# Gated linear attention in a two-block forward pass: the chunk states of the second pair move into VectorE's turn of the first

## The reference, cut to what matters

```python
def step(S, inp):
    qj, kj, vj, laj = inp
    bcum = jnp.cumsum(laj, axis=2)
    ...
    o = jnp.einsum('bhls,bhse->bhle', attn, vj) + jnp.einsum('bhld,bhde->bhle', qj * jnp.exp(bcum), S)
    btot = bcum[:, :, -1:, :]
    S_new = jnp.exp(btot[:, :, 0, :])[..., None] * S + jnp.einsum('bhld,bhle->bhde', kj * jnp.exp(btot - bcum), vj)
    return S_new, o
```

## Time and profile before

| what | us |
|---|---|
| median of 3 runs | 2453.25 |
| lowest and highest | 2450.51, 2454.04 |
| the profiled execution | 2450.63 |
| its span, first to last instruction | 2448.9 |
| TensorE busy in it (matmul) | 2334.7 |
| VectorE busy | 1200.1 |
| ScalarE busy | 944.2 |
| GpSimd busy | 820.0 |
| mean granted TensorE clock | 0.983 |

### The profile page before, as it was taken

One profiled execution on the slowest core, in us unless ns is written; L12 is line 12 of the kernel. 1 busy time (PEld: TensorE's weight loads), 2 busy tenths in 40 slices (PEclk: granted clock), 3 DMA queues, 4 the chain that ended last, 5 costly groups with the idle time before them and its releaser, 6 DMA issues. The chain is left out here.

```text
span 2448.9 us, 37685 instructions
## 1 busy us (share of the span) xinstructions
PE 2334.7 (95%) x15896; PEld 1796.9 (73%) x15896; DVE 1200.1 (49%) x1957; ACT 944.2 (39%) x1351; POOL 820.0 (33%) x369
## 2 busy tenths in 40 slices
PE   7999999998999999999989989998999999999997
PEld 5776677776877857777768768887766678888885
DVE  3353754343234528544342777674454476406434
ACT  4432345444244223553352433333346523212243
POOL 2342133323433412333234432221332344444442
PEclk9999999999999999999999999998999999999999
DMA  3221122222222202222123200001121222222222
GB/s 131 95 86 44 61 78 69 69 70 69 96 72 77 95 26 70 76 69 74 65 70 115 96 19 4 3 4 62 63 76 52 69 94 100 99 95 95 98 99 70
DMA packets 50564, 176.19 MB, mean 72 GB/s; under 512 B 5780, under 2 KB 6748, under 8 KB 50396
## 3 DMA queue, kind: packets, MB, share of 16 engines
q1 hardware_dynamic: 50396, 173.78, 21.2%
HBM read 171.65 MB, written 2.11 MB: 71 GB/s over the span
## 5 line engine op out<-in xcount | busy, mean ns | idle before, releaser
L356 POOL TENSOR_TENSOR w_low<-work,w_high 128x1024 fp32r<-128x1024 f32 x309 | 753.0, 2437 | 1348.2 <-ACT w_high L300 1348.2
L283 PE MATMUL ps<-x_high_tiles,w_high 128*128 128x512 f32 x1560 | 633.0, 406 | 21.1 <-ACT x_high_tiles L329 5.7
L300 ACT ACTIVATE w_high<-work 128x1024 fp32r<-128x1024 f32 x309 | 326.9, 1058 | 754.3 <-PE ps L283 750.2
L283 PE MATMUL ps<-x_low_tiles,w_high 128*128 128x512 f32 x1560 | 611.9, 392 | 2.8 <-DVE x_low_tiles L399 2.0
L283 PE MATMUL ps<-x_high_tiles,w_low 128*128 128x512 f32 x1560 | 611.8, 392 | 0.0
L283 PE MATMUL ps<-arena_parts,w_high 128*128 128x512 f32 x1264 | 399.7, 392 | 13.5 <-POOL w_low L356 5.5
L283 PEld LDWEIGHTS ps<-x_high_tiles,w_high 128*128 128x128 f32 x1560 | 295.1, 189 | 128.0 <-issue 59.5
L283 PEld LDWEIGHTS ps<-x_low_tiles,w_high 128*128 128x128 f32 x1560 | 294.7, 189 | 69.4 <-DVE x_low_tiles L399 4.2
L283 PEld LDWEIGHTS ps<-x_high_tiles,w_low 128*128 128x128 f32 x1560 | 295.3, 189 | 63.5 <-issue 5.5
L283 PEld LDWEIGHTS ps<-arena_parts,w_high 128*128 128x128 f32 x1264 | 238.0, 188 | 67.4 <-issue 8.6
L283 PE MATMUL ps<-arena_parts,w_low 128*128 128x512 f32 x608 | 237.3, 390 | 0.0
(11 more groups left out here) (451 smaller groups left out, 2816.4 us busy)
## 6 DMA issues: line engine op xcount, KB each, us to landing
work<-w_first SPq DMA_DIRECT2D x180, 512.0 KB, 3.5
work<-w_second SPq DMA_DIRECT2D x134, 512.0 KB, 3.5
xT_sb<-xT SPq DMA_DIRECT2D x8, 256.0 KB, 5.1
outT<-arena SPq DMA_DIRECT2D x8, 256.0 KB, 2.1
arena<-distance_bias SPq DMA_DIRECT2D x4, 256.0 KB
small<-small SPq DMA_DIRECT2D x1, 815.5 KB, 4.5
arena<-consts SPq DMA_DIRECT2D x1, 544.0 KB, 3.7
base<-consts SPq DMA_DIRECT2D x1, 512.0 KB
```

Source lines behind the costliest of these rows:

```text
L283: ins = pe.matmul(out, lhsT, rhs, start=(n == 0 and k == 0 and q == 0), stop=(n == unit["granules"] - 1 and k == len(ops[i]) - 1 and q == 2))
L300: act.activation(m.wh[:, split_of(g), :], m.raw[:, raw_of(g), :], ACT.Copy).then_inc(sem["high_ready"], 1)
L356: pool.tensor_tensor(m.wl[:, split_of(g), :], m.raw[:, raw_of(g), :], m.wh[:, split_of(g), :].bitcast(F32), ALU.subtract).then_inc(sem["lo ...
```

## The change

The chunk states of pair r=0 no longer end VectorE's turn: pair r=1 follows in the same turn. Pairs r=2 and r=3 take the turns that r=1 and r=2 had. The closing wait has one turn more, so that the outputs stay in the turn in which they are. The instructions are the same, and so is every wait on a semaphore; TensorE's and ScalarE's programs are not touched. It applies to both hybrid layers.

```diff
                     if a == 0:
                         own.op(ins)
                 ins.then_inc(sem["state_ready"], 1)
-            yield
-        yield from turns(5)
+            if r:
+                yield
+        yield from turns(6)
         for h in range(GLA_H):
             dve.wait_ge(sem["gla_rstd"], h + 1)
             x = attn[:, h, :]
```

## The result

The changed kernel takes 2437.36 us (median of 4 runs, 2432.66 to 2438.79) against 2453.14 us (4 runs, 2450.51 to 2454.04). The ratio is 0.9936, with a 95% interval of 0.9924 to 0.9948: 15.8 us, or 0.64%, faster. The forecast was 2438.6 us.

A forecast was written before the change was run, and what follows sets the result against it. TensorE is busy 95% of the span, so time is won only where it stands still or runs slowly. 2.69 + 2.93 + 1.71 = 7.33 us a layer, 14.66 for two, from the median 2453.25 gives 2438.6 us; range 2433 to 2446.

The forecast's parts named there:

- The stop at granule 38: Middle of granule 38: TensorE's 2.69 us wait for state 4 goes whole in each layer.
- The low clock: TensorE's products right behind the 2.69 us idle: return to the high clock level wins 2.93 us a layer.
- The stop at read 7: Last state read, L1206: TensorE's wait for state 7 goes, 1.71 us a layer.
- The wait ahead of the evacuations: VectorE, pair r=1 before granule 37's first evacuation: later evacuation costs nothing, margin 1.1 us before granule 38's first product.
- GpSimd: State pairs beside w_low: r=1 runs free, collisions of r=2 or r=3 would cost zero.
- The splits: Three L593 of VectorE's turn 38 run some 2 us after r=2's wait; reader at granule 44, cost zero.
- the later waits of the stage: Waits for w_low (1.8 us) and L593 (2.4 us) near the stage's end: move along unshortened.
- the slower rival: Stage's later gaps, 1.8 and 2.4 us: low clock moves there, 2.93 us each at four gaps, 2456.2 us; chance 0.03.
- The rival of a late evacuation: Granule 38 starts late, L283 waiting for L456: 1.1 us a layer, 2440.8 us, or 2446.6 with low clock; chance 0.07.

The follow-up runs named there:

- the pads: Changed kernel with 1, 4 or 7 added VectorE operations between pair r=1 and the evacuation behind it: 2432.73, 2440.72 and 2446.94 us.
- four pads: Changed kernel with four added VectorE operations (2.86 us) between pair r=1 and the evacuation behind it: 2440.72 us, ratio 0.9957.

## Why the prediction was right

By the steps of its list:

1. *The stop at granule 38* goes whole. Pair r=1 ends at 1191.13 + 0.48 = 1191.61, 1.95 us after its sums; 1.98 us was taken from r=2. It is 4.7 us ahead of the sums that need it (1196.28), as forecast.
2. *The low clock* was won, and undersized by little: 3.08 us a layer (r=1 alone moved) against 2.93 us.
3. *The stop at read 7* costs 1.80 us (r=3 alone moved) against 1.71 us.
4. *The wait ahead of the evacuations* costs nothing. The margin was put at 1.1 us; the trace shows 1.25 and the pads 1.24 us.
5. *GpSimd.* The scaling of r=2 was expected at 0.4 us after the end of w_low and comes at 0.43 us; that of r=3 has 0.18 us. None is long.
6. *The splits* follow r=2 and nobody waits for them at that place.

The sum was 14.66 us; the stage shows 15.07 us, the medians 15.8 us with an interval of 12.8 to 18.6 us. How close the forecast came, 1.2 us, is in part luck. It carried over the 2.6 us by which the profiled execution lay under the median before; after, the profiled execution is 0.5 us above the median.

One sentence failed: that the later waits of the stage move along unshortened. In the second layer the low clock came back behind the 1.82 us wait for w_low, which is the place that the slower rival had named. Timeline and a stretch of the changed kernel:

```profile
1249.72 0.50 PE L283 MATMUL ps<-arena_parts,w_high 128*128 128x512 f32 x1 [1.82 <-POOL w_low L356]
...
1257.90 0.47 PE L283 MATMUL ps<-arena_parts,w_high 128*128 128x512 f32 x1 [0.85 <-DVE arena_parts L593]
```

```profile
1251.00:1252.00 1.00, 1.00 (x3) 0.79 (x3) 1.00 (x1) 0.00 (x0) 1.00 (x1) 0.50 0.87 299
```

It cost nothing there, and that is one thing that the rival had missed. The products behind that gap end in a wait for the outputs of VectorE, which TensorE's pace does not bring sooner. The slow products took up time that was waited before: the wait for L593 is 0.85 us in place of 2.4, and from the first L1243 to the first L694 the two kernels take 113.6 and 113.5 us. The changed kernel run again shows it in the first layer: there the clock fell behind the wait for w_low, that for L593 was 0.86 us in place of 2.48, and L1243 to the norm took 91.79 us against 91.80 without the fall.

The rival's mechanism is real one gap further on. Behind the wait for L593 nothing took up the slow products: where the clock fell there (r=1 alone, r=3 alone, old turns with the sum in PSUM, four pads) each layer paid 1.6 us, not the 2.93 us that the rival had put. None of the profiled executions of the changed kernel has that fall. Why the fall comes behind one gap in one kernel and behind the other in the next stays open, so that the change escapes this cost is a reading of the traces and not something that the prediction foresaw.

The rival of a late evacuation was told apart by the pads: its place was right, and its price without the clock (the lateness less the margin), and the kernel stands 1.25 us in front of it.

## What to carry to other kernels

Where an engine's program is an order written by hand, look in the timeline for work that is ready and stands behind something of a later time: here 1.98 us of VectorE's work, free to start at 1199.1 us, was held until 1204.4 us by an evacuation that ScalarE had not yet released. Before moving it forward, read off how long what it is put ahead of can wait, and check that number with added operations; it is the whole risk. A stop of the busiest engine is priced with its clock: here idle 2.69 us, clock 3.08 us. Then follow what was won past the next waits: r=1 alone won 11.5 us in its two stages and kept 8.3 us of them.

## What the runs showed of the hardware that was not expected

The low clock also came behind a stop of only 0.77 us; that the stop was its cause is not shown. In the second layer of the kernel with the old turns and the sum in PSUM, TensorE had waited 0.77 us at 1199.31 and then ran small products; the clock of the next stretch:

```profile
1201.00:1202.00 1.00, 1.00 (x15) 0.88 (x14) 1.00 (x3) 0.00 (x0) 0.00 (x0) 0.73 0.83 258
```

0.73 is a mean over the fall from the 2.4 GHz level to the 1.2 GHz level. Its stage is 38.44 us there and 36.88 us in the first layer, where the same stop left the clock at 1.00: 1.56 us for the same work. Waits of 1.71 us (before) and 1.62 us (four pads) left it up; one of 1.82 us (changed kernel, 1249.72) did not, while the wait of 1.83 us at the same place of its first layer (594.95) left it at 1.00, and the wait for L593 behind it was 2.48 us as ever. That wait of 2.48 us in its turn left the clock up here and was followed by the fall with r=1 alone. The length of a stop alone therefore does not tell. The Trainium skill (TensorE: Matmul & The Clock Gate, Why this matters for your kernels) warns only of idle gaps longer than all of these; the rows contradict it as a bound, here as at the 2.69 us.

What stays open is the 2 to 5 us by which medians of kernels with the same stage differ. In the profiles the falls of the clock stand at other places from one kernel to the next. The times go with the granted clock of the whole execution: of 39 executions of the kernel before, in three jobs, the eight at 0.980 took 2454.7 to 2456.3 us and the three at 0.985 and 0.986 took 2446.5 to 2448.8 us. That the falls make up the whole difference was not tried.
